# An fp32 decoder layer on one core: the sums of up weights get semaphores of their own and are split behind the weights

## The reference

```
def swiglu(h, w_gate, w_up, w_down):
    return (jax.nn.silu(h @ w_gate) * (h @ w_up)) @ w_down

for layer in range(DEPTH):          # DEPTH is 1
    h = rms_norm(x, norm_mix[layer])
    x = x + hybrid_mixer(h, ...)
    h = rms_norm(x, norm_ffn[layer])
    x = x + swiglu(h, w_gate[layer], w_up[layer], w_down[layer])
return rms_norm(x, norm_final)
```

## Time and profile before

| | |
|---|---|
| runs | 1379.26, 1379.51, 1391.07 us, median 1379.51 |
| the profiled execution | 1378.64 us, span 1376.9 us |
| PE busy | 1362.5 us, 99% |
| DVE busy | 922.5 us, 67% |
| ACT busy | 702.5 us, 51% |
| read from HBM | 257.33 MB, 188 GB/s over the span |

### The profile page before, as it was taken

One profiled execution on the slowest core, in us unless ns is written; L12 is line 12 of the kernel. 1 busy time (PEld: TensorE's weight loads), 2 busy tenths in 40 slices (PEclk: granted clock), 3 DMA queues, 4 the chain that ended last, 5 costly groups with the idle time before them and its releaser, 6 DMA issues.

```text
span 1376.9 us, 26434 instructions
## 1 busy us (share of the span) xinstructions
PE 1362.5 (99%) x11280; PEld 1325.5 (96%) x11280; DVE 922.5 (67%) x1192; ACT 702.5 (51%) x913; POOL 44.9 (3%) x70
## 2 busy tenths in 40 slices
PE   8999999999999999999999999999999999999997
PEld 7888999999999999999999999999999999999997
DVE  5554557667655657666787888875446778887554
ACT  6343356656545655465645554544334455545444
POOL 3000010000000110000000000000000000000111
PEclk9999999999999999999999999999999999999999
DMA  7776655444565666546556655565555565666653
GB/s 241 246 231 219 186 171 156 140 152 146 154 192 168 194 203 218 184 168 201 165 182 194 217 181 181 182 214 208 191 198 184 184 214 169 193 196 231 210 198 123
DMA packets 135264, 261.08 MB, mean 190 GB/s; under 512 B 8448, under 2 KB 25408, under 8 KB 134768
## 3 DMA queue, kind: packets, MB, share of 16 engines
q1 hardware_dynamic: 132912, 251.13, 57.0%
q0 software_dynamic: 1792, 7.57, 1.6%
q10 hardware_dynamic: 448, 0.76, 0.2%
HBM read 257.33 MB, written 2.10 MB: 188 GB/s over the span
## 4 chain that ended last, share of the span: by engine, by line
PE 88%; DVE 7%; ACT 2%; DMA 2%; issue 1%; ACTq 0%; DVEq 0%
PE bank L646 24%; PE bank L647 23%; PE bank L648 23%; PE bank L885 4%; PE bank L887 4%; PE bank L888 4%; DVE weight_lo_ring L1322 2%; PE bank L634 2%; DVE weight_sums_lo L1342 1%; ACT weight_hi_ring L1071 1%; DMA raw_ring<-in_w_up 1%; DVE weight_sums L1331 1%; PE bank L784 1%; DVE act_rows L1382 1%; PE bank L695 1%
## 5 line engine op out<-in xcount | busy, mean ns | idle before, releaser
L1322 DVE TENSOR_TENSOR weight_lo_ring<-raw_ring,weight_hi_ring 128x1024 fp32r<-128x1024 f32 (+2 forms) x479 | 579.9, 1221 | 319.2 <-ACT weight_hi_ring L1071 263.9
L1071 ACT ACTIVATE weight_hi_ring<-raw_ring 128x1024 fp32r<-128x1024 f32 (+2 forms) x431 | 446.2, 1047 | 343.4 <-PE bank L648 271.0
L646 PE MATMUL bank<-weight_hi_ring,hT_hi 128*128 128x256 f32 (+2 forms) x1276 | 380.9, 298 | 0.0
L648 PE MATMUL bank<-weight_hi_ring,hT_lo 128*128 128x256 f32 (+2 forms) x1276 | 375.5, 294 | 0.0
L647 PE MATMUL bank<-weight_lo_ring,hT_hi 128*128 128x256 f32 (+2 forms) x1276 | 375.5, 294 | 0.0
L646 PEld LDWEIGHTS bank<-weight_hi_ring,hT_hi 128*128 128x128 f32 x1276 | 239.8, 188 | 10.0 <-issue 3.4
L647 PEld LDWEIGHTS bank<-weight_lo_ring,hT_hi 128*128 128x128 f32 x1276 | 239.9, 188 | 6.1
L648 PEld LDWEIGHTS bank<-weight_hi_ring,hT_lo 128*128 128x128 f32 x1276 | 239.6, 188 | 6.3
L646 PE MATMUL bank<-weight_hi_ring,h2T_hi 128*128 128x256 f32 x704 | 196.5, 279 | 3.2 <-DVE weight_lo_ring L1322 3.1
L648 PE MATMUL bank<-weight_hi_ring,h2T_lo 128*128 128x256 f32 x704 | 195.3, 277 | 0.0
L647 PE MATMUL bank<-weight_lo_ring,h2T_hi 128*128 128x256 f32 x704 | 195.3, 277 | 0.0
(11 more groups left out here) (253 smaller groups left out, 1897.0 us busy)
## 6 DMA issues: line engine op xcount, KB each, us to landing
raw_ring<-in_w_in SPq DMA_DIRECT2D x96, 512.0 KB, 3.4
raw_ring<-in_w_gate SPq DMA_DIRECT2D x88, 512.0 KB, 4.3
raw_ring<-in_w_up SPq DMA_DIRECT2D x88, 512.0 KB, 4.2
raw_ring<-in_w_down SPq DMA_DIRECT2D x88, 512.0 KB, 3.9
raw_ring<-in_w_in SPq DMA_DIRECT2D x55, 480.0 KB, 4.2
raw_ring<-in_w_out SPq DMA_DIRECT2D x32, 512.0 KB, 4.0
raw_ring<-in_w_br_c SPq DMA_DIRECT2D x16, 256.0 KB, 3.9
raw_ring<-in_w_br_a SPq DMA_DIRECT2D x16, 256.0 KB, 6.8
```

The lines of the kernel that those rows point to most:

```text
L646: pe.matmul(dst, x_hi, w_hi, start=opening, stop=False, skip_group_check=True)
L648: m = pe.matmul(dst, x_lo, w_hi, start=False, stop=last and k == UK - 1, skip_group_check=True)
L1071: act.activation(whi[:, s, :, 0:width(u)], raw[:, s, :, 0:width(u)], ACT.Copy)\
L1322: dve.tensor_tensor(lo, w, hi.bitcast(F32), ALU.subtract).then_inc(lo_ready, 1)
```

## The change

ACT splits the weights of an up unit with seven products first and counts up `hi_ready`, and then the sums, with a semaphore of their own, `ext_hi_ready`. DVE subtracts for the weights first and counts up `lo_ready`, waits for `ext_hi_ready`, subtracts for the sums and counts up `ext_ready`. PE waits for `ext_ready` in the middle of such a unit, ahead of the three products that use the sums, and DVE waits for it before it overwrites `weight_sums`. Apart from this, DVE handles the low parts of the transposed activation three units later (`ACT_LO_AT`), except for the last chunk of each half.

```diff
--- before.py
+++ after.py
@@ -118,6 +118,7 @@
 UP_END = {AT["up", i, UPC - 1]: i for i in range(NC_F)}
 ACT_T_AT = {AT[("down", (h, 0), 5) if i == b - 1 else ("gate", i + 1, 5)]: i
             for h, (a, b) in enumerate(HALVES) for i in range(a, b)}
+ACT_LO_AT = {v if i + 1 in (b for _, b in HALVES) else v + LAG: i for v, i in ACT_T_AT.items()}
 KD_H = [2 * (b - a) for a, b in HALVES]
 DOWN_END = {AT["down", (h, c), KD_H[h] - 1]: (h, c) for h in range(2) for c in range(NC_D)}
 LAST_DOWN = (1, NC_D - 1)
@@ -417,6 +418,8 @@
         h_sum_hi = sem("h2_sums_hi_ready")
         h_sum_lo = sem("h2_sums_ready")
         w_summed = sem("weights_summed")
+        ext_hi_ready = sem("weight_sums_hi_ready")
+        ext_ready = sem("weight_sums_ready")
         silu_ready = sem("silu_ready")
         p_copied = sem("products_copied")
         up_emptied = sem("up_banks_emptied")
@@ -918,6 +921,7 @@
                 into(i, 3, 0, block(1, 0), quarters(u, 1, 0), False)
                 into(i, 2, 0, total(3), quarters(u, 1, 1), False)
                 into(i, 6, 1, total(1), quarters(u, 0, 1), True)
+                pe.wait_ge(ext_ready, N_SEVEN[u] + 1)
                 into(i, 7, 0, total(0), extra(0), True)
                 into(i, 7, 1, total(2), extra(1), True)
                 return into(i, 2, 1, block(1, 1), extra(2), False)
@@ -1061,15 +1065,16 @@
                 if u >= RING:
                     act.wait_ge(unit_used, u - RING + 1)
                 if is_seven(u):
-                    n = N_SEVEN[u]
-                    act.wait_ge(w_summed, n + 1)
-                    if n >= 2:
-                        act.wait_ge(unit_used, SEVENS[n - 2] + 1)
-                    act.activation(ext_hi[:, n % 2, :, :], t_sum[:, :, :], ACT.Copy)
+                    act.wait_ge(w_summed, N_SEVEN[u] + 1)
                 else:
                     act.wait_ge(raw_ready[s], landed(u))
                 act.activation(whi[:, s, :, 0:width(u)], raw[:, s, :, 0:width(u)], ACT.Copy)\
                    .then_inc(hi_ready, 2 if u == 1 else 1)
+                if is_seven(u):
+                    n = N_SEVEN[u]
+                    if n >= 2:
+                        act.wait_ge(unit_used, SEVENS[n - 2] + 1)
+                    act.activation(ext_hi[:, n % 2, :, :], t_sum[:, :, :], ACT.Copy).then_inc(ext_hi_ready, 1)
 
             def split_in_loop(u0, rounds, units, cols=W):
 
@@ -1326,7 +1331,7 @@
                 n = N_SEVEN[u]
                 dve.wait_ge(raw_ready[u % RING], landed(u))
                 if n >= 1:
-                    dve.wait_ge(lo_ready, SEVENS[n - 1] + 1)
+                    dve.wait_ge(ext_ready, n)
                 quarter = raw[:, u % RING, :, :].rearrange("p k (c n) -> p (k c) n", c=2)
                 chain(dve.tensor_tensor(t_sum[:, 0:2, :], quarter[:, 1:2, :].to_broadcast([P, 2, Q4]), quarter[:, 0:4:3, :],
                                         ALU.subtract))
@@ -1336,11 +1341,12 @@
             def split(u):
                 if is_seven(u + 1) and not is_seven(u):
                     sums_of_weights(u + 1)
+                split_unit(u % RING, u + 1, width(u))
                 if is_seven(u):
-                    e = N_SEVEN[u] % 2
-                    dve.wait_ge(hi_ready, u + 1)
-                    dve.tensor_tensor(ext_lo[:, e, :, :], t_sum[:, :, :], ext_hi[:, e, :, :].bitcast(F32), ALU.subtract)
-                split_unit(u % RING, u + 1, width(u))
+                    n = N_SEVEN[u]
+                    dve.wait_ge(ext_hi_ready, n + 1)
+                    dve.tensor_tensor(ext_lo[:, n % 2, :, :], t_sum[:, :, :], ext_hi[:, n % 2, :, :].bitcast(F32),
+                                      ALU.subtract).then_inc(ext_ready, 1)
                 if is_seven(u + 1) and is_seven(u):
                     sums_of_weights(u + 1)
 
@@ -1504,8 +1510,8 @@
                     last.then_inc(emptied["dve"], 1)
                 if v in UP_END:
                     up_rows(v, UP_END[v])
-                if v in ACT_T_AT:
-                    lo_of_act(ACT_T_AT[v])
+                if v in ACT_LO_AT:
+                    lo_of_act(ACT_LO_AT[v])
                 if v in DOWN_END:
                     add_down(v, *DOWN_END[v])
                 mixer_step(v - U_MIX)
```

## The result

| | before | after |
|---|---|---|
| median of the runs, us | 1380.35 (4 runs, 1379.26 to 1391.07) | 1365.87 (4 runs, 1365.78 to 1367.45) |
| ratio, 95% interval | | 0.9881 [0.9831, 0.9930] |
| profiled execution, us (span) | 1378.64 (1376.9) | 1365.83 (1364.1) |

A forecast was written before the change was run, and what follows sets the result against it. TensorE (PE), busy 99% of the span, was taken as the bound. Pauses 7.3 plus slow pace 4.1 less 0.4 us gave 11.0 us: profiled 1367.6, plus 0.9 to the median, 1368.5 us; range 1367.0 to 1376.5 us.

The forecast's parts named there:

- its two kinds: Gate, up and down stage: PE pauses for the weights' low parts, 7.3 us; matmuls at 117.6 instead of 113.3 ns, 4.1 us.
- the new chain of 9.9 us: DVE's work from the up rows to gate unit 7's low parts: 9.9 us where 11.6 stood.
- the free met wait: PE's new wait for the sums in mid-unit, already met when reached: cost taken as 0.
- the met wait that costs: Rival: 55 restarts of PE at 0.11 us give 6.1 us back, 1374.6 us; chance 0.12.
- the rival that is slower: Rival: PE's mid-unit waits leave the slow pace behind throughout the stage, +21 us, 1400 us; chance 0.04.
- only the pauses go: Rival: PE's pauses, 7.3 us, vanish but the slow pace stays, 1372.2 us; chance 0.24.
- 0.4 us for restarts: Deduction from the stage's gain: transposes and single restarts of PE keep some 0.4 us.
- ten of eleven chunks: Claim that ten of the eleven column chunks have the DVE order seen between the up rows and gate unit 7.
- part 4: DVE's low parts of the activation three units later in nine chunks: two subtractions of 0.68 us leave gate unit 7's chain.
- late elsewhere: Rival: DVE or a load is late at another place, half or all the gain returns, 1374 to 1380 us; chance 0.10.
- my cover of 0.8 us: DVE reaches the sums for the next up unit 4 some 14.7 us behind the up rows instead of 15.5.
- parts 1 and 2: ACT splits weights first, high parts 0.85 us earlier; DVE subtracts for weights first, releasing PE 0.96 us earlier.

The follow-up runs named there:

- 205 further waits: Changed kernel with a further, long-met wait of PE in the middle of 205 units (172 gate and down, 33 ordinary up): 1366.66 us, ratio 0.9890.
- the delays: Useless DVE additions ahead of gate unit 7's low parts in four chunks: changed kernel 1375.78 us; with activation low parts at their old place and fewer additions 1370.56 us.
- the kernel with four pauses: Changed kernel with three, four, six and nine useless DVE additions ahead of gate unit 7's low parts in four chunks: 1375.78 us, ratio 0.9956.

## Why the prediction was wrong

**Right.** The loss of the stage, 11.6 us, and its two kinds (7.3 and 4.1 us in the prediction, 6.9 and 4.7 by the starts); the new chain of 9.9 us, measured as 9.9; the free met wait; that no pause and no slow pace would be left. The 205 further waits exclude the met wait that costs and, with 6268 matmuls, the rival that is slower; 6264 matmuls in the changed kernel exclude that only the pauses go.

**Wrong: the low end of the range.** Counting back from the profiled execution, 1378.64 - 11.6 = 1367.0 us is what the change gives if it recovers the whole loss and all else stays. That was the low end, so it left nothing for the rest of the kernel, which moves by up to 1.5 us from one execution to the next and was 1.1 us shorter in the profile after. The forecast itself then held back 0.4 us for restarts and added 0.9 us to go from the profiled execution to the median of the runs. Both terms were mis-sized. The stage gained 11.7 us and not 11.0: the restarts behind transposes are in the full pace already (780 to 800 us has one group of them and 179 matmuls). And the 0.9 us is no constant between a profile and a median. It depends on how much the kernel before happens to lose in an execution, which its three profiles put down mostly to the slow pace; its runs go from 1373.9 to 1388.4 us in the experiments, and the longer ones were not profiled. A change that removes pauses removes this spread too, so its time is to be reckoned from the full pace (1366.4), not from the median of the kernel before. The 2.6 us between forecast and result are roughly 0.9 of the median, 0.7 in the stage and 1.1 of chance, by which the stage began at 646.45 instead of 647.55 us. The chance alone does not explain the miss: in the second profile of the changed kernel the stage began at 647.29 us, and its 1366.68 us still lie below the range. For the same reason the statement that no more than 11.6 us can be won was wrong of the medians, which lie 14.5 us apart in the first measurement.

**Wrong: ten of eleven chunks.** The pattern of the earlier trace rows stands in nine. The first chunk of each half has no up rows ahead of its gate unit 7, and that of the second half shows no pause in any profile. The sum does not change by it, since it counts matmuls.

**Wrong: the share of part 4.** I let the later low parts bring 1.36 of the 1.7 us in the chain to gate unit 7. They bring 1.0 us, and nothing of the time: without them the orders leave 0.4 us to spare. What they bring is a reserve of 1.4 us in place of 0.4, shown by the delays. Alone they move the lateness to gate unit 1 of the next chunk, the rival "late elsewhere" in a kernel where the orders give DVE no room; my cover of 0.8 us (14.7 us instead of 15.5; measured 14.3) was that of the whole change.

**Not seen:** that neither of parts 1 and 2 shortens the time alone. I had priced them as two gains of 0.85 and 0.96 us. The first is DVE's idle time and needs both; the second is a release that was never late once the idle time had gone.

## What to carry to other kernels

Where an engine is at its full pace but for short pauses, count its instructions in equal stretches; a view of idle time misses what modelled ends cover, here all but 3.1 of 11.6 us. Where one engine makes two results in turn and a second one works on both, the second should be able to begin on the first result while the other is made: that takes the same order on both engines and a count for each result. Turning round only one of the two engines gained nothing here. A term that removes a random loss is to be taken from the level without it, and a range needs the spread of the untouched part.

## What the runs showed of the hardware

- **A second pace of PE at the same clock.** At a granted clock of 1.00, streams of matmuls with 256 columns came either every 113.3 or every 117.6 ns, the latter for 31 to 85 us at a time or only for the rest of the one unit (2 to 3 us) behind a pause. In this stage no slow stretch occurred in the six profiles without a pause, and each one in the others began at a pause or a narrow miss of 0.03 us; most pauses had none behind them. A group of transposes ended nearly all the long stretches, though not always the first group; short ones ended at the next unit. What sets it off or ends it is open.
- **The clock fell behind a pause of 2.78 us.** In the kernel with four pauses PE stood 2.8 us and ran at the 2.4 GHz level for 1.1 us, and then came a stretch at half the clock, the 1.2 GHz level:

```profile
1190.00:1194.00 4.00, 1.49 (x14) 1.00 0.04 14
1195.20:1198.50 3.30, 3.30 (x18) 0.51 0.92 292
1199.00:1203.00 4.00, 4.00 (x38) 1.00 0.50 148
```

```profile
1194.11 0.38 PE L650 MATMUL bank<-weight_hi_ring,h2T_hi 128*128 128x256 f32 x1 [2.62 <-DVE weight_lo_ring L1328]
...
1195.70 0.41 PE L652 MATMUL bank<-weight_hi_ring,h2T_lo 128*128 128x256 f32 x1
1195.91 0.41 PE L650 MATMUL bank<-weight_hi_ring,h2T_hi 128*128 128x256 f32 x1
```

Starts lie 0.21 us apart there; 15 matmuls at 0.1 us more are 1.5 us, a surcharge of half on that pause. The pause of 1.39 us had none. The Trainium skill (TensorE: Matmul & The Clock Gate, "The HAM clock gate") says that an idle engine falls back to 1.2 GHz and that activity releases it; the trace agrees in the two levels and in that the fall follows on idle time. It is one event in one profile.
